# Token-ordered, evenly spread input of the seven-product feed-forward, and a later start of the weight sums

## What is computed

```python
for l in range(DEPTH):                       # DEPTH = 2, SEQ = 512, D_MODEL = 1024
    h = rms_norm(x, g_mix[l])
    z = h @ w_in[l]                          # 10752 columns, split among the mixers and gates
    ...                                      # retention ya, spatial gating yb, dilated attention yc
    merged = (gt[:, :, 0] * (ya @ w_branch[l, 0]) + gt[:, :, 1] * (yb @ w_branch[l, 1])
              + gt[:, :, 2] * (yc @ w_branch[l, 2]))
    x = x + merged @ w_o[l]
    h = rms_norm(x, g_ffn[l])
    gate, up = jnp.split(h @ w_gate_up[l], 2, axis=-1)      # 2816 columns each
    x = x + (jax.nn.silu(gate) * up) @ w_down[l]
```

## Time and profile before

| | before |
|---|---|
| median of 3 runs | 1963.01 us (1962.14 to 1964.38) |
| the profiled execution | 1963.38 us, its span 1961.6 us |
| TensorE: matmuls, weight loads | 1917.3 us (98%), 1712.7 us |
| VectorE, ScalarE, POOL busy | 1249.1 us (64%), 855.1 us (44%), 97.1 us (5%) |
| mean granted clock of TensorE | 0.992 |
| a weight slab: high part L1004, low part L1204 | 1057 ns, 1221 ns, 396 each |
| queues: loads (q1), POOL's (q0) | 218.49 MB, 75.51 MB |

### The profile page before, as it was taken

How to read it: one execution, slowest core, us unless ns; L and a number is a source line. 1 busy time by engine, 2 the same in 40 slices (tenths; PEclk the granted TensorE clock), 3 DMA queues, 4 the chain that set the end, 5 groups by cost and what they waited for, 6 DMA issues and landing times. The chain is left out here.

```text
span 1961.6 us, 26697 instructions
## 1 busy us (share of the span) xinstructions
PE 1917.3 (98%) x10664; PEld 1712.7 (87%) x10664; DVE 1249.1 (64%) x1633; ACT 855.1 (44%) x1194; POOL 97.1 (5%) x148
## 2 busy tenths in 40 slices
PE   6999999999999989999999999999999999999999
PEld 5888888888888889899988888888888887998998
DVE  5666666755666687357566666677466667763775
ACT  4444533434334455245445444445233444542554
POOL 1111111111111100000000000000000000000000
PEclk9999999999999999999999999999999999999999
DMA  8767877788777766356433223223333332553663
GB/s 283 193 172 178 183 175 203 198 212 216 186 203 196 196 187 197 115 161 194 140 109 88 78 76 87 82 81 91 100 100 96 101 99 86 167 167 97 204 201 132
DMA packets 85897, 295.68 MB, mean 151 GB/s; under 512 B 20368, under 2 KB 20624, under 8 KB 84624
## 3 DMA queue, kind: packets, MB, share of 16 engines
q1 hardware_dynamic: 73104, 218.49, 35.9%
q0 software_dynamic: 12672, 75.51, 17.1%
HBM read 291.79 MB, written 77.66 MB: 188 GB/s over the span
## 5 line engine op out<-in xcount | busy, mean ns | idle before, releaser
L1004 ACT ACTIVATE w_high<-raw 128x1024 fp32r<-128x1024 f32 x396 | 418.2, 1057 | 812.6 <-PE bank L816 672.9
L816 PE MATMUL bank<-h_high,w_high 128*128 128x512 f32 x1472 | 574.4, 390 | 20.2 <-DVE h_low L1209 12.8
L1204 DVE TENSOR_TENSOR w_low<-raw,w_high 128x1024 fp32r<-128x1024 f32 x396 | 482.8, 1221 | 129.7 <-ACT w_high L1004 122.5
L816 PE MATMUL bank<-h_low,w_high 128*128 128x512 f32 x1472 | 562.6, 382 | 0.0
L816 PE MATMUL bank<-h_high,w_low 128*128 128x512 f32 x1472 | 562.5, 382 | 0.0
L816 PEld LDWEIGHTS bank<-h_high,w_high 128*128 128x128 f32 x1472 | 281.4, 191 | 65.6 <-issue 10.8
L816 PEld LDWEIGHTS bank<-h_high,w_low 128*128 128x128 f32 x1472 | 281.0, 191 | 40.7
L816 PEld LDWEIGHTS bank<-h_low,w_high 128*128 128x128 f32 x1472 | 281.4, 191 | 39.0
L816 PE MATMUL bank<-in_high,w_high 128*128 128x512 f32 x672 | 255.0, 379 | 0.0
L816 PE MATMUL bank<-in_low,w_high 128*128 128x512 f32 x672 | 254.7, 379 | 0.0
L816 PE MATMUL bank<-in_high,w_low 128*128 128x512 f32 x672 | 254.7, 379 | 0.0
(11 more groups left out here) (153 smaller groups left out, 2255.0 us busy)
## 6 DMA issues: line engine op xcount, KB each, us to landing
raw<-weights SPq DMA_DIRECT2D x325, 512.0 KB, 3.8
weight_sums<-weights POOLq DMA_DIRECT2D x108, 512.0 KB, 5.9
raw<-weight_sums SPq DMA_DIRECT2D x72, 512.0 KB, 3.6
weight_sums<-weight_sums POOLq DMA_DIRECT2D x36, 512.0 KB, 4.2
turned<-rows SPq DMA_DIRECT2D x3, 768.0 KB, 6.7
xT<-x_t SPq DMA_DIRECT2D x8, 256.0 KB, 7.1
decay_sb<-decay SPq DMA_DIRECT2D x8, 256.0 KB, 4.3
out_t<-xT SPq DMA_DIRECT2D x8, 256.0 KB, 6.3
```

The lines of the kernel that those rows point to most:

```text
L816: return pe.matmul(o, w, m, start=start, stop=stop)
L1004: act.activation(w_high[:, PART_SLOT[s], :, :], raw[:, s % RAW_SLOTS, :, :], ACT.Copy).then_inc(part_high_w.sem, 1)
L1204: dve.tensor_tensor(w_low[:, PART_SLOT[s], :, :], raw[:, s % RAW_SLOTS, :, :], w_high[:, PART_SLOT[s], :, :], ALU.subtract).then_inc(part_ ...
```

## The change

The diff does two things.

First, the quick units' input is in token order: `normed` is [channel block, token], read and written without a stride; a quarter takes 256 tokens in a row. The order in which TensorE sees the tokens is then another (of a half, token t and t + 128 in turn), the output of the quick units has it too, the plain tiles' output `f` is stored to match (`bank_order`, `by_quarters`), and the evacuation of `down` puts the tokens in order again as it reads PSUM. The steps that prepare the input are dealt out anew: seven `normed` and an eighth over the posts of `fup` 0, `fgate` 1 and `fup` 1, the sums and parts one or two per tile behind them; s4, `a12`'s low part and `a22` go into the first quick unit.

Second, POOL waits for the evacuation of `rv` 0 of the first layer before its first copy.

```diff
-    post[AT["fup", 0, 0]] += [("normed", n) for n in range(4)]
-    post[AT["fgate", 0, 1]] += [("normed", n) for n in range(4, KT)]
-    post[AT["fup", 0, 1]] += [("part_high", "a11"), ("part_low", "a11"), ("input_sum", "s1")]
-    post[AT["fgate", 0, 2]] += [("input_sum", "s2"), ("part_high", "s2"), ("part_low", "s2")]
-    post[AT["fup", 0, 2]] += [("part_high", "s1"), ("part_low", "s1"), ("input_sum", "s3")]
-    post[AT["fgate", 0, 3]] += [("part_high", "s3"), ("part_low", "s3"), ("input_sum", "s4"), ("part_high", "s4"),
-                                ("part_low", "s4")]
-    post[AT["fup", 0, 3]] = [("part_high", "a12"), ("part_low", "a12")] + post[AT["fup", 0, 3]]
-    post[AT["quick", PLAIN_PAIRS, A11B11]] += [("part_high", "a22"), ("part_low", "a22")]
+    post[AT["fup", 0, 0]] += [("normed", n) for n in range(3)]
+    post[AT["fgate", 0, 1]] += [("normed", n) for n in range(3, 7)]
+    post[AT["fup", 0, 1]] += [("normed", 7), ("part_high", "a11"), ("part_low", "a11")]
+    post[AT["fgate", 0, 2]] += [("input_sum", "s1"), ("input_sum", "s2"), ("part_high", "s2")]
+    post[AT["fup", 0, 2]] += [("part_low", "s2"), ("part_high", "s1")]
+    post[AT["fgate", 0, 3]] += [("part_low", "s1"), ("input_sum", "s3"), ("part_high", "s3")]
+    post[AT["fup", 0, 3]] = [("part_high", "a12"), ("part_low", "s3")] + post[AT["fup", 0, 3]]
+    post[AT["quick", PLAIN_PAIRS, A11B11]] += [("part_low", "a12")]
+    post[AT["quick", PLAIN_PAIRS, S2T2]] += [("input_sum", "s4"), ("part_high", "s4"), ("part_low", "s4")]
+    post[AT["quick", PLAIN_PAIRS, S1T1]] += [("part_high", "a22"), ("part_low", "a22")]
...
-        normed = over("normed", in_high_at + 4 * row_bytes, [P, KT, 4, P], F32)
+        normed = over("normed", in_high_at + 4 * row_bytes, [P, KT, SEQ], F32)
...
+        def bank_order(stored):
+            return stored.rearrange("p (i t a) -> p i a t", i=2, a=2)
+
+        def by_quarters(tokens):
+            return tokens.rearrange("p (i a t) -> p i a t", i=2, a=2)
...
-            return normed[:, 4 * k:4 * k + 4, :, :].rearrange("p k (r i) q -> p k i r q", i=2)[:, :, i, :, :]
+            return normed[:, 4 * k:4 * k + 4, 2 * P * i:2 * P * (i + 1)]
...
+            pool.wait_ge(tile_stored.sem, tile_stored.at(0, AT["rv", 0]))
             for layer in range(DEPTH):
                 for n, u in enumerate(QUICK_UNITS):
...
-                        act.activation(halves(parts(key)[0]), parted(src), ACT.Copy).then_inc(high_ready.sem, 1)
+                        dst = parts(key)[0]
+                        if key[0] == "f":
+                            act.activation(bank_order(dst), by_quarters(src), ACT.Copy).then_inc(high_ready.sem, 1)
+                        else:
+                            act.activation(halves(dst), parted(src), ACT.Copy).then_inc(high_ready.sem, 1)
...
-                        elif t[0] in ("wo", "down"):
+                        elif t[0] == "down":
+                            x = by_quarters(xT[:, t[-1], :])
+                            dve.tensor_tensor(x, src.rearrange("p (t a i) -> p i a t", a=2, i=2), x, ALU.add).then_inc(
+                                tile_stored.sem, 1)
+                        elif t[0] == "wo":
                             dve.tensor_tensor(xT[:, t[-1], :], src, xT[:, t[-1], :], ALU.add).then_inc(tile_stored.sem, 1)
...
-                        dve.scalar_tensor_tensor(normed[:, n, :, :], xT[:, n, :].rearrange("p (q m) -> p m q", m=4),
-                                                 vec[:, n:n + 1], norm_rstd[:, :].rearrange("p (q m) -> p m q", m=4),
+                        dve.scalar_tensor_tensor(normed[:, n, :], xT[:, n, :], vec[:, n:n + 1], norm_rstd[:, :],
                                                  ALU.mult, ALU.mult).then_inc(normed_ready.sem, 1)
```

More of the change, by code:

```diff
@@ L617, in quarter @@
             i, k = int(name[1]) - 1, int(name[2]) - 1
-            return normed[:, 4 * k:4 * k + 4, :, :].rearrange("p k (r i) q -> p k i r q", i=2)[:, :, i, :, :]
-        def as_quarter(stored):
-            return stored.rearrange("p k (r q) -> p k r q", r=2)
+            return normed[:, 4 * k:4 * k + 4, 2 * P * i:2 * P * (i + 1)]
         def input_source(name):
@@ L626, in input_source @@
                 return quarter(name)
-            return {"s1": as_quarter(input_sum[:, 0, :, :]), "s2": as_quarter(input_sum[:, 1, :, :]),
+            return {"s1": input_sum[:, 0, :, :], "s2": input_sum[:, 1, :, :],
                     "s3": quarter("a21"), "s4": quarter("a11")}[name]
@@ L1148, in _ @@
                             act.wait_ge(input_summed.sem, input_summed.at(base, name))
-                        act.activation(as_quarter(input_parts(name)[0]), input_source(name), ACT.Copy).then_inc(
+                        act.activation(input_parts(name)[0], input_source(name), ACT.Copy).then_inc(
                             part_high.sem, 1)
@@ L1371, in _ @@
                         high, low = input_parts(name)
-                        dve.tensor_tensor(as_quarter(low), input_source(name), as_quarter(high),
-                                          ALU.subtract).then_inc(part_low.sem, 1)
+                        dve.tensor_tensor(low, input_source(name), high, ALU.subtract).then_inc(part_low.sem, 1)
                     elif kind == "rotate":
@@ L1393, in _ @@
                             dve.tensor_tensor(lo, src.rearrange("p (a n) -> p a n", a=2), hi, ALU.subtract).then_inc(
+                                low_ready.sem, 1)
+                            continue
+                        if key[0] == "f":
+                            dve.tensor_tensor(bank_order(lo), by_quarters(src), bank_order(hi), ALU.subtract).then_inc(
                                 low_ready.sem, 1)
```

## The result

The changed kernel takes 1950.3 us (median of 4, 1948.2 to 1954.1) against 1963.7 (1962.1 to 1965.2): 0.9934 of the kernel before, 95% interval 0.9914 to 0.9954. It gained 13 us where 29 were forecast (1933.7 against 1963.0). The profiled execution was the slowest of its four, 1954.05 us with a span of 1952.3.

The account below looks back on a forecast made before the run. TensorE was taken as the bound, so only its waits and half-clock windows count. Span 1961.6 - 16.6 - 14.1 - 5.0 + 6.0 + 0.4 = 1932.3 us, timed as 1933.7; 8-in-10 range 1924 to 1953.

Parts of the forecast that it names:

- start: Kernel's first 30 us: without POOL's copies the first loads land sooner, 5.0 us saved, bounds 0 and 8.
- first attention: First layer's attention: without POOL the `probs` waits and half-clock windows go, 14.1 us saved, bounds 9 and 15.
- feed-forward order: Feed-forward of both layers: waits before `fup` 2 and (s2, t2) go, 16.6 us saved, bounds 12 and 19.
- The wait for a12: Product (a12, b21) in each layer: a12's low part comes late in VectorE's queue, a wait of 1.9 us stays.
- `normed` at 750 ns: VectorE's `normed` without a stride: some 750 ns in place of 1560; 16 of them save 13 us of VectorE.
- the `down` evacuation at 0.69 us: VectorE's 32 evacuations of `down`, reading PSUM at a step of four: 0.69 us taken, upper bound 1.09.
- the 0.4 us for the boundary: Last `down` tile, awaited by the next layer or final store: slower evacuation, 0.4 us counted, at most 3 x 0.4.
- the step of two of L1396: PSUM read costing 692 ns: said to stay on an 8-byte line, so not contradicting a 0.8 us stride price for `down`.
- the price of POOL's traffic on the first layer's products: First layer's seven products: POOL's moved traffic delays weight loads, 6 us lost over 63 tiles, bounds 0 and 21.
- (A): Rival: first layer's product loads late as a rule, mean landing 6.6 us, +15 us, 1949; chance 0.18.
- The 1.5 us that POOL adds: Loads in the first layer's products: 4.0 plus POOL's 1.5 gives a 5.5 us landing, just free against 5.6.
- The 21 us named as the upper bound of the term: First layer's products: at a mean landing of 6.6 us, (6.6+2.4)/3 - 2.68 = 0.33 us over 63 tiles.

Follow-up runs that it names:

- the order alone: Changed kernel without its added POOL wait, so new order and layout with POOL starting at once: 1944.5 us, 0.9908 of the kernel before.
- the pause: Changed kernel with POOL waiting for `rv` 0 of each layer, not only of the first: 1927.6 us, 0.9823 of the kernel before.
- the late start alone: Kernel before with only POOL's start put behind `rv` 0 of the first layer: 1970.4 us, 1.0048 of the kernel before.

## Why the prediction was wrong

The terms that save were right in the profile. Profile against sum: start 5.0 against 5.0, first attention 13.9 against 14.1, feed-forward order 15.9 against 16.6 (and 15.7 us in time, by the order alone).

The match of the attention's term is in part luck: the version with the order alone runs the same code up to 650 us, and its profile had 7.2 us there where that of the kernel before had 15.2.

The wait for a12 was foreseen at 1.9 us per layer and is 1.9 from start to start (2.01 less 0.11), at 686.66 and 1666.89 us. What was not foreseen is 0.8 us in the next unit. `normed` at 750 ns and the `down` evacuation at 0.69 us were right; the gap at the layer's end is 0.69 us as before, so the 0.4 us for the boundary weren't needed.

The Trainium skill (SBUF — State Buffer, Door 1) gives PSUM lines of 8 bytes, two float32 values, and names a price of patterns that are not contiguous for matmuls. The prediction carried that over to VectorE's read of PSUM, though not into its sum; 32 reads at 691 ns show nothing of it. Its remark that the step of two of L1396 stays on such a line was wrong, since two float32 values are 8 bytes: the 692 ns of that row already spoke against the price.

The step that failed is the price of POOL's traffic on the first layer's products: 6 us were counted, 23 were measured between the changed kernel and the one with the pause. From start to start the first layer's feed-forward behind the first unit costs 26.9 us in the profile of the changed kernel, which was the slowest of its runs, 23.6 in a second profile, and 1.9 with the pause. The nearest rival is (A), 1949 against 1950.3, with a chance of 0.18, but its nearness is in part luck: it wanted a mean landing of 6.6 us, and the means were 6.1 and 5.8. (The half of the DMA engines that (A) gives to POOL doesn't stand in the earlier trace rows; the trace of the kernel before has 0.48 at 300 to 650 us. In the products after the change both queues together take 0.87.) Two things in that step were off:

- The landing. The 1.5 us that POOL adds were read where one load comes per 5.2 us, and were used where one comes per 2.7. In place of 5.5 the mean was 6.1, with 12 of 29 loads over 6 us in the second stretch, while 5.6 were free.
- The tail. A mean that is "just free" was priced by the mean. Before, a load lay ready 1.5 to 2.2 us (median by stretch) until ScalarE split it; after, the median was 0.5, and for 22 of 53 loads the split began within 0.3 us of the landing. Then a longer landing delays the split, and a short one gives little back, since a slot's next load is issued only behind its split. From issue to the end of the low part a load took 9.4 and 9.7 us in the two stretches, against 9.0 and 8.7 with the pause. The clock windows at the two longest waits add 5.1 us by the count.

The 21 us named as the upper bound of the term was by its own formula for a mean of 6.6. At the measured mean that formula gives (6.1+2.4)/3 - 2.68 = 0.15 x 63 = 10 us, and 3 us at the 5.8 of the second profile, whose cost was 23.6. So the mean alone explains less than half. That the rest is spread and clock is what the waits suggest; no run varied the spread alone. POOL's end came later than the 991 us foreseen (its last transfer is issued at 1017.5) and still did not reach the second layer's first exchange.

That the loads are late because of POOL is shown: the pause removes it, the late start alone brings it. How much of it is the DMA engines' time, the memory's bandwidth or the kind of transfer stays open. The estimate by the bandwidth figure of the Trainium skill's page DMA: Bandwidth & Descriptors (Specifications) gave 27 us and came near to 23. By the same page of the Trainium skill (Bandwidth) the figure is a core's share while both cores of a pair stream, and here one core runs. The stretches moved 253 GB/s where 10 to 30 us of the kernel before had moved 352, making the transfers single, with the same bytes, took 7 us away, and with copies for adds 289 GB/s went with half the cost. So no row here shows the limit itself at work. Whether a fourth slot for `raw` would hide the landings wasn't tried.

## What to carry to other kernels

Traffic that leaves a sensitive place goes somewhere: find the stretch with the shortest time per load on its new way and put the background work where the loads are sparse, here behind `rv` 0 in each layer, which turns a gain of 13 us into one of 35 (0.982). Price a transfer's delay by the slack of one slot, from landing to first use, and by its long cases, not by its mean against a mean: here the slack's median was 1.5 to 2.2 us and POOL added 2 to the mean landing, and the waits came. A wait named after an engine's evacuation may be a late load further up in that engine's queue: look at what the releaser itself waited for before reordering it.

## What the runs showed of the hardware

- In the changed kernel, beside the loads, two adding transfers of 512 KB that POOL started together took 10.5 us (mean) and one without another of POOL's 7.2, against 6.0 and 4.5 for copies of the same size, all between places of device memory.
- Loads of 512 KB, one per 2.7 us, landed in 4.0 us (mean) without POOL's transfers and in 6.1 and 5.8 beside them, in two profiles of the changed kernel.
- VectorE's evacuation from PSUM took 691 ns at a step of four elements and 691 without one; the same step on two SBUF inputs had cost `normed` 1560 against 749.
- In the changed kernel's products TensorE's granted clock was 0.50 (1.2 GHz) at the gaps of 3.4 and 4.1 us from start to start, for 3.4 and 6.8 us (the second time from 910.0, 1.9 us before TensorE went on), and stayed at 1.00 behind the two of 2.6 us. The length of a gap does not settle it: with the evacuations ahead of the splits, gaps of 2.3 us at 728 and 862 us had the half clock behind them, for 3.4 us each, and in the late start on the kernel before two of 3.1 us, at 666 and 1654 us, had none. The prediction counted no clock window behind waits of up to 3.0 us, from one such wait.
